# A decoder layer with a mixture of experts: the last three scatters patched by marking matrices counted per token tile, and a fourth tile read before the last scatter

## The chip, the cores and the metric

The kernel runs on one core of a Trainium2 chip. The metric is the device time of one execution in microseconds (us), as the median of three runs.

## The reference

One layer on x of shape (1, 1024, 1024), all float32: attention, then a hierarchical mixture of experts, then a final norm. What matters here is its end:

```python
gates = jnp.sum(jax.nn.one_hot(eid, N_EXPERTS) * top_w[..., None], axis=1)   # two experts of 32 per token
y = jnp.zeros_like(h)
for e in range(N_EXPERTS):
    hid = jax.nn.silu(jnp.dot(h, w_gate[e])) * jnp.dot(h, w_up[e])
    y = y + gates[:, e:e + 1] * jnp.dot(hid, w_down[e])
x = x + gate_m[:, None] * y
...
return rms_norm(x, g_final)
```

Each token's row of 1024 values goes to two experts, and the final norm needs both results of a token.

## The kernel before

The 1024 tokens are 8 token tiles of 128 rows (tile 0 to tile 7). After attention and routing, the work on the experts goes in `NSTEP` = 20 steps, called lists here. A list holds up to 128 rows, in four groups of 32, for one to four experts. For list n, GpSimd (POOL) gathers the rows of the tokens from memory (`gather`, line 760), TensorE (PE) turns them and multiplies them with the weights (`turn_rows`, `gate_up`, `turn_hidden`, `down_proj`), ScalarE (ACT) and VectorE (DVE) evacuate, `ev_y` on DVE (lines 1603 and 1606) weighs the result and adds the token's x where this is its first expert, and POOL scatters the rows into the table `expert_rows` in memory (`scatter`, line 767). The table (`y_dram`) has 2048 rows: one for each token's first expert, and one for its second.

At the end, the two rows of each token are read back, added, normed and written to the output. Most tiles do this by DMA: two reads of 512 KB by `expert_rows` (line 617), an addition on DVE (`combine`, line 1691), the sum of squares on ACT (line 1080), a small addition and a power of -0.5 on POOL (lines 826 and 827), the scaling on DVE (`finish`, line 1700), and a write of 512 KB from SyncE (SP, line 664). These reads wait for `rows_out`, which POOL raises once every scatter has landed.

Tiles 0, 1 and 2 (`AHEAD` = 3) don't wait for the last three lists, 17, 18 and 19 (`NLATE` = 3, `LATE` = 17). Their rows are read once the scatters up to list 16 have landed (line 630), while lists 18 and 19 are still being computed. Their rows in lists 17 to 19 aren't scattered (the index is set out of bounds). Instead, PE adds them: for each such tile and late list, DVE makes a 128x128 matrix of zeros and ones (a mark, line 1664), and a product of the mark with the list's rows, which are still in SBUF, puts each row at its token (`add_into`, line 2222). A product with the identity adds the rows that were read, once DVE has added their two halves (line 1685). Sum of squares and scaling of these tiles read PSUM. They are the tiles in `mixed`.

The order of the end is written out by hand: `read` is the order of the reads behind `rows_out`, `last` the order in which ACT, POOL and the writes of SP take the tiles, and a list of calls at line 1703 the order of `combine` and `finish` on DVE. Each engine runs its instructions in the order of the program, and SP's queue holds both the reads and the writes of the output.

Of the kernel before, what the change touches and what calls it, by code (L numbers as in the profile page):

```python
# [11 lines left out]
ALU = mybir.AluOpType  # L12
# [53 lines left out]
def hybrid_layer(nc, x, c, w_ada, b_ada, g_attn, w_in, g_kv, w_uk, w_uv, lam_q1, lam_k1, lam_q2, lam_k2,  # L66
# [88 lines left out]
    with ctx:  # L155
# [153 lines left out]
        def dist(t):  # L309
# [83 lines left out]
        marks = [mark_room[NLATE * i:NLATE * (i + 1)] for i in range(AHEAD)]  # L393
        zero_rows = W7[:, D:2 * D]
        iota_tok = BIAS[:, 2, 0:P]
        late_tok = logits[:, :, :].rearrange("p t n -> p (t n)")[:, 2 * NT + 5 * T + NLATE:2 * NT + 5 * T + NLATE * (1 + AHEAD)].rearrange(
            "p (i j) -> p i j", j=NLATE)
# [63 lines left out]
        def scattered(b):  # L461

            return len(range(b, LATE, 2))
# [14 lines left out]
        def _(sp):  # L478
# [140 lines left out]
            for n in range(NSTEP + 1):  # L619
# [4 lines left out]
                if n >= 1:  # L624
# [16 lines left out]
            with sp.If(n_ov > 0):  # L641
# [12 lines left out]
                sp.wait_ge(yg_ahead, 64 * AHEAD)  # L654
# [14 lines left out]
        def _(pool):  # L669
# [94 lines left out]
            def scatter(n):  # L764

                pool.wait_ge(y_sb, 2 * n + 2)
                pool.indirect_dma_start(out=y_dram, out_offset=bass.IndirectOffsetOnAxis(
                                            ap=dst_rows[:, n:n + 1].bitcast(U32), axis=0), in_=held[n % HELD], in_offset=None,
                                        bounds_check=2 * S - 1, oob_is_err=False
                                        ).then_inc(y_out[n % 2] if n < LATE else y_last, 16)  # L770
# [31 lines left out]
            pool.wait_ge(yg_ahead, 32 * AHEAD)  # L802
# [5 lines left out]
            with pool.If(n_ov > 0):  # L808
# [3 lines left out]
                pool.wait_ge(y_last, 16 * NLATE)  # L812
# [8 lines left out]
            pool.wait_ge(y_last, 16 * NLATE)  # L821
# [9 lines left out]
        def _(act):  # L831
# [238 lines left out]
            for n, t in enumerate(last):  # L1070
                if t in mixed:
                    i = mixed.index(t)
                    act.wait_ge(mix_ps, i + 1)
                    whole = PS[:, 2 * i:2 * i + 2, :].rearrange("p a n -> p (a n)")
# [10 lines left out]
        def _(dve):  # L1085
# [566 lines left out]
            for n in range(NSTEP):  # L1652
# [9 lines left out]
                if 3 <= n < 3 + NLATE * AHEAD:  # L1662
# [593 lines left out]
```

## Time and profile before

| | |
|---|---|
| time, median of 3 runs | 997.08 us (996.19 to 998.70) |
| the profiled execution's own time | 995.87 us |
| its span in the trace | 994.1 us |
| granted TensorE clock, mean | 0.992 of full speed |
| busy: PE, DVE, ACT, POOL | 947.6, 630.1, 398.3, 120.3 us |

The span runs from the first instruction to the last. The profiled execution took 1.8 us more than its span, and it was 1.2 us under the median. Busy shares are of the whole span, while all that the change moves at the end lies in the last 50 us.

### The profile page before, as it was taken

Reading aid. Unit: us, or ns where it says so; the run is one execution under the profiler, and the core shown is the slowest. Engines: PE = TensorE matmul, PEld = TensorE weight load, DVE = VectorE, ACT = ScalarE, POOL = GpSimd, SP = SyncE. Lnnn points to the kernel's source line nnn. Section 1 sums busy time; section 2 is a strip of 40 time slices with the busy share of each in tenths; the row PEclk is TensorE's granted clock in tenths of the full one; section 3 lists DMA queues with packets and bytes.
Section 4 is the critical chain, followed back from the end, with each engine's and each line's share of the span. In section 5 each row is a group of like instructions: output and inputs, shape, how many; then the busy total and the mean of one; then the engine's idle time right before and its main releaser. Section 6 shows DMA issues by size and latency. Waiting matters only on the chain.

```text
span 994.1 us, 15197 instructions
## 1 busy us (share of the span) xinstructions
PE 947.6 (95%) x5400; PEld 520.1 (52%) x5400; DVE 630.1 (63%) x1670; ACT 398.3 (40%) x901; POOL 120.3 (12%) x221
## 2 busy tenths in 40 slices
PE   3899999999999999999999999999899999999895
PEld 2455476444446856667776555555634433344342
DVE  3378646999999799887777423345724444444356
ACT  6131134676671188877668412121211221111103
POOL 2101000000005711110000000000111111111114
PEclk9899999999999999999999999999999999999998
DMA  9998100101103100040000410059899999999979
GB/s 324 328 358 298 43 22 22 44 21 43 43 22 107 69 1 1 2 171 23 2 2 1 156 57 37 27 212 404 312 411 421 393 423 420 420 420 421 420 307 372
DMA packets 70093, 188.37 MB, mean 189 GB/s; under 512 B 10280, under 2 KB 37216, under 8 KB 57728
## 3 DMA queue, kind: packets, MB, share of 16 engines
q1 hardware_dynamic: 61888, 169.48, 44.6%
q0 software_dynamic: 5760, 16.33, 4.2%
q10 hardware_dynamic: 2368, 1.57, 0.5%
q8 instruction: 44, 0.72, 0.3%
q14 instruction: 33, 0.27, 0.1%
HBM read 169.98 MB, written 22.04 MB: 193 GB/s over the span
## 4 chain that ended last, share of the span: by engine, by line
PE 53%; DVE 20%; DMA 16%; issue 6%; POOL 3%; ACT 1%; SPq 0%; DVEq 0%; POOLq 0%; ACTq 0%
DMA expert_rows<-HT,SC 12%; PE PS L2018 11%; DVE BIAS L1222 8%; PE PS L1911 6%; PE PS L2148 5%; PE PS L1954 5%; PE PS L1976 4%; PE PS L1872 3%; PE PS L2171 3%; PE PS L1824 3%; PE PS L1971 2%; DVE X L1286 2%; PE PS L1849 2%; PE PS L1789 2%; DMA HT<-h_rows,SC 2%
## 5 line engine op out<-in xcount | busy, mean ns | idle before, releaser
L1824 PE MATMUL PS<-HT,X 128*128 128x512 f32 x384 | 168.8, 593 | 0.0
L1824 PEld LDWEIGHTS PS<-HT,X 128*128 128x128 f32 x384 | 72.5, 190 | 92.4 <-issue 92.2
L936 ACT ACTIVATE X<-X,nmx 128x128 f32<-128x128 f32 (+7 forms) x128 | 98.4, 770 | 51.7 <-DVE nmx L1286 51.4
L2018 PE MATMUL PS<-QKV,HT 128*128 128x512 f32 x256 | 113.7, 597 | 0.0
L1222 DVE TENSOR_SCALAR_CACHE_REDUCE BIAS<-SC,W 128x384 f32<-128x384 f32 (+3 forms) x128 | 96.4, 810 | 1.1
L2148 PE MATMUL PS<-QKV,HT 128*32 128x512 f32 (+1 forms) x528 | 91.9, 594 | 2.8 <-ACT HT L1034 1.2
L919 ACT ACTIVATE X<-SC,W 128x896 f32<-128x896 f32 x64 | 69.6, 1088 | 43.1 <-DVE W L1210 43.1
L1594 DVE TENSOR_TENSOR HT<-PS,HT 128x256 f32<-128x256 f32 x20 | 8.5, 425 | 123.3 <-ACT HT L1042 123.3
L1911 PE MATMUL PS<-QKV 64*128 64x512 f32 (+3 forms) x384 | 79.0, 517 | 1.6 <-DVE nmx L1286 1.1
L2018 PEld LDWEIGHTS PS<-QKV,HT 128*128 128x128 f32 x256 | 47.4, 190 | 53.7 <-issue 53.6
L1954 PE MATMUL PS<-ident,X 128*128 128x128 f32 x432 | 63.2, 279 | 2.2 <-DVE X L1304 2.1
L1042 ACT ACTIVATE HT<-PS 128x256 f32<-128x256 f32 x20 | 7.7, 383 | 132.2 <-PE PS L2148 125.5
L1286 DVE CUSTOM_DVE_ANT_0 X<-PS,R 128x128 f32<-128x128 f32 (+7 forms) x80 | 50.8, 674 | 14.6 <-PE PS L1911 8.6
L2148 PE MATMUL PS<-SC,HT 128*32 128x512 f32 (+1 forms) x160 | 56.4, 593 | 0.0
L1286 DVE CUSTOM_DVE_ANT_0 X<-PS,SC 128x1024 f32<-128x1024 f32 (+5 forms) x48 | 42.0, 887 | 17.9 <-PE PS L1911 17.8
L1954 PEld LDWEIGHTS PS<-ident,X 128*128 128x128 f32 x432 | 47.3, 141 | 11.4 <-issue 8.6
L1911 PEld LDWEIGHTS PS<-QKV 64*128 64x128 f32 x384 | 31.6, 185 | 27.8 <-issue 20.6
L2148 PEld LDWEIGHTS PS<-QKV,HT 128*32 128x32 f32 (+1 forms) x528 | 24.6, 111 | 36.9 <-issue 34.0
L760 POOL DMA_INDIRECT HT<-h_rows,SC x20 | 20.6, 1029 | 188.9 <-DMA expert_rows<-HT,SC 132.2
L1114 DVE SCALAR_TENSOR_TENSOR QKV<-QKV,cact 128x512 f32<-128x512 f32 x56 | 42.1, 752 | 2.0
L1971 PEld LDWEIGHTS PS<-QKV,HT 128*128 128x128 f32 x288 | 34.5, 191 | 16.6 <-issue 9.2
L2148 PE MATMUL PS<-X,HT 128*32 128x512 f32 (+1 forms) x112 | 42.3, 593 | 0.0
(335 smaller groups left out, 1590.4 us busy)
## 6 DMA issues: line engine op xcount, KB each, us to landing
QKV<-in_w_down_dram SPq DMA_DIRECT2D x20, 1024.0 KB, 26.4
QKV<-in_w_gate_dram SPq DMA_DIRECT2D x19, 1024.0 KB
QKV<-in_w_up_dram SPq DMA_DIRECT2D x19, 1024.0 KB
QKV<-in_w_ada_dram SPq DMA_DIRECT2D x8, 2048.0 KB, 12.7
QKV<-in_w_ada_dram SPq DMA_DIRECT2D x8, 1024.0 KB, 12.5
X<-in_w_in_dram SPq DMA_DIRECT2D x16, 512.0 KB, 3.8
X<-in_w_down_dram SPq DMA_DIRECT2D x8, 1024.0 KB
W<-in_w_gate_dram SPq DMA_DIRECT2D x5, 1024.0 KB
```

Source lines behind the costliest of these rows:

```text
L919: act.activation(RL[:, n % 2, 0:w], SC[:, sc_off[t]:sc_off[t] + w], ACT.Sign, bias=tk[:, 4, i:i + 1].bitcast(F32), scale=-1.0, accum_out=c ...
L936: act.activation(sc, sc, ACT.Exp, bias=nmx[:, i % 4, m:m + 1], scale=-1.0, accum_out=rs[:, i, m:m + 1]).then_inc(exp_done, 1)
L1114: link(dve.scalar_tensor_tensor(out=w[:, 0, :], in0=w[:, j, :], scalar=cact[:, j:j + 1], in1=w[:, 0, :], op0=ALU.mult, op1=ALU.add))
L1222: dve.tensor_scalar(BIAS[:, i % 3, 0:w], SC[:, sc_off[t]:sc_off[t] + w], thr.bitcast(F32)[:, i:i + 1], 0.0, ALU.is_lt, ALU.add, accum_out= ...
L1286: dve.tensor_tensor_reduce(sc_buf[i % 4][:, m, 0:w], PS[:, 2 * m:2 * m + 2, :].rearrange("p a n -> p (a n)")[:, BANK * n:BANK * n + w], aw ...
L1824: end = pe.matmul(PS[:, 2 * b + half, :], WS[:, b, j, :], HT[:, j, BANK * half:BANK * (half + 1)], start=(j == 0), stop=(j == KC - 1))
L1911: end = pe.matmul(PS[:, 2 * m + n + c0 // BANK, 0:c1 - c0], QKV[rows_m, q0:q0 + P], QKV[rows_m, k0 + c0:k0 + c1], start=True, stop=True)
L1954: end = pe.transpose(PS[:, 4 + g % 2, c0:c0 + P], sc_buf[i % 4][:, m, P * b:P * (b + 1)], ident[:, :])
L1971: end = pe.matmul(PS[:, 6 + h % 2, slot], turned_at(i)[:, g % 4, P * (b - b0):P * (b - b0 + 1)], vf[:, u * S + P * b:u * S + P * (b + 1)], ...
L1976: end = pe.matmul(PS[DH * m:DH * (m + 1), 6 + h % 2, slot], vd[:, b, v0:v0 + DH], turned_at(i)[:, g % 4, c0:c0 + P], start=(b == 0), stop= ...
L2018: end = pe.matmul(PS[:, n % 4, :], HT[:, k, P * (n // 2):P * (n // 2 + 1)], wo[:, k, BANK * (n % 2):BANK * (n % 2 + 1)], start=(k == 0), s ...
L2148: end = pe.matmul(PS[at, 2 + b, :], hgT[b][:, P * c_ + at.start:P * c_ + at.stop], WGU[w][:, c_, :, :], start=(c_ == 0), stop=(c_ == KC - 1))
```

## The change

Marks are now counted per tile. `first_late` = (0, 1, 1, 2) gives for tiles 0 to 3 the first late list that is patched by a mark: tile 0 has marks for lists 17, 18 and 19, tiles 1 and 2 for lists 18 and 19, tile 3 for list 19 alone. These are 8 marks instead of 9. Tiles 1 and 2 are read after scatter 17 has landed, tile 3 after scatter 18, and tile 3 is then combined on DVE as before, and only then completed in PSUM by PE. The scatters of lists 17 and 18 count on the alternating semaphores, and each waits for the scatter two before it. `last`, `mixed` and the order of calls on DVE are new.

```diff
-        AHEAD, NLATE = 3, 3
+        AHEAD, NLATE, PATCHED = 3, 3, 4
+        first_late = (0, 1, 1, 2)
-        last = (0, 3, 4, 1, 5, 6, 2, 7)
-        mixed = (0, 1, 2)
+        last = (0, 4, 1, 5, 3, 6, 2, 7)
+        mixed = (0, 1, 3, 2)
...
         def scattered(b):
-            return len(range(b, LATE, 2))
+            return len(range(b, NSTEP - 1, 2))
...
-            for t in range(AHEAD):
+            for t in range(PATCHED):
                 for k in range(2):
                     row = S * k + P * t
                     sp.dma_start(y_dram[row:row + P, :], zero_rows).then_inc(yg_ahead, 16)
...
                     if n == LATE:
                         for b in range(2):
-                            sp.wait_ge(y_out[b], 16 * scattered(b))
+                            sp.wait_ge(y_out[b], 16 * len(range(b, LATE, 2)))
                         for t in range(AHEAD):
-                            expert_rows(t, yg_ahead)
+                            if first_late[t] == 0:
+                                expert_rows(t, yg_ahead)
+                    if n == LATE + 1:
+                        sp.wait_ge(y_out[1], 16 * scattered(1))
+                        for t in range(AHEAD):
+                            if first_late[t] == 1:
+                                expert_rows(t, yg_ahead)
...
             sp.sem_inc(tables_set, 1)
+            sp.wait_ge(y_out[0], 16 * scattered(0))
+            for t in range(AHEAD, PATCHED):
+                expert_rows(t, yg_in[read.index(t)])
             sp.wait_ge(rows_out, 1)
-            for i, t in enumerate(read):
-                expert_rows(t, yg_in[i])
+            for t in range(PATCHED, T):
+                expert_rows(t, yg_in[read.index(t)])
...
                 pool.wait_ge(y_sb, 2 * n + 2)
+                if LATE <= n < NSTEP - 1:
+                    pool.wait_ge(y_out[n % 2], 16 * (n // 2))
...
-            link(dve.tensor_scalar(late_dst, PS[:, 2, LATE:NSTEP], P * AHEAD + 0.5, None, ALU.is_ge))
+            for j in range(NLATE):
+                link(dve.tensor_scalar(late_dst[:, j:j + 1], PS[:, 2, LATE + j:LATE + j + 1], P * tiles_of[j] + 0.5, None,
+                                       ALU.is_ge))
...
-            link(dve.tensor_copy(late_tok[:, 0, :], PS[:, 2, LATE:NSTEP]))
-            for i in range(1, AHEAD):
-                link(dve.tensor_scalar(late_tok[:, i, :], PS[:, 2, LATE:NSTEP], float(-P * i), None, ALU.add))
+            for i, f in enumerate(first_late):
+                link(dve.tensor_scalar(late_tok[:, tok_col[i]:tok_col[i] + NLATE - f], PS[:, 2, LATE + f:NSTEP], float(-P * i),
+                                       None, ALU.add))
...
             finish(0)
             combine(3)
             combine(4)
+            finish(4)
+            combine(5)
+            finish(1)
+            finish(5)
+            combine(6)
             finish(3)
-            combine(5)
-            finish(4)
-            finish(1)
-            combine(6)
-            finish(5)
+            finish(6)
             combine(7)
-            finish(6)
             finish(2)
             finish(7)
...
-            for i in range(AHEAD):
-                for j in range(NLATE):
-                    pe.wait_ge(marked, NLATE * i + j + 1)
+            pe.wait_ge(marked, len(mark_of))
+            for t in mixed:
+                for j in range(first_late[t], NLATE):
                     pe.wait_ge(y_sb, 2 * (LATE + j + 1))
-                    add_into(i, marks[i][j], held[(LATE + j) % HELD], j == 0, False)
-                pe.wait_ge(marked, NLATE * AHEAD + i + 1)
-                add_into(i, ident[:, :], yg[i][0], False, True).then_inc(mix_ps, 1)
+                    add_into(mix_banks[t], marks[(t, j)], held[(LATE + j) % HELD], j == first_late[t], False)
+                if t < AHEAD:
+                    pe.wait_ge(marked, len(mark_of) + t + 1)
+                else:
+                    pe.wait_ge(cb_done, read.index(t) + 1)
+                add_into(mix_banks[t], ident[:, :], yg[t][0], False, True).then_inc(mix_ps, 1)
```

SP's queue, from the last weight load to the first write of the output, the part for more than the planned rows left out. `X<-expert_rows` are reads of tiles 0 to 2, `QKV<-expert_rows` those of tiles 3 to 7, `y_out0` and `y_out1` count the landed scatters of even and odd lists. Before:

```order
L450 DMA QKV<-in_w_down_dram 128x2048
L617 DMA X<-expert_rows 128x1024 [waits dn_ps,y_out0,gu_ps,y_out1]
L617 DMA X<-expert_rows 128x1024 x5
L634 TENSOR_LOAD ovi [waits dn_ps,gu_ps,route_done]
...
L617 DMA QKV<-expert_rows 128x1024 [waits rows_out]
L617 DMA QKV<-expert_rows 128x1024 x9
L664 DMA out_dram<-X 128x1024 [waits fin_done]
```

And now:

```order
L455 DMA QKV<-in_w_down_dram 128x2048
L622 DMA X<-expert_rows 128x1024 [waits dn_ps,y_out0,gu_ps,y_out1]
L622 DMA X<-expert_rows 128x1024
L622 DMA X<-expert_rows 128x1024 [waits y_out1,dn_ps,gu_ps]
L622 DMA X<-expert_rows 128x1024 x3
L645 TENSOR_LOAD ovi [waits dn_ps,route_done,gu_ps]
...
L622 DMA QKV<-expert_rows 128x1024 [waits y_out0]
L622 DMA QKV<-expert_rows 128x1024
L622 DMA QKV<-expert_rows 128x1024 [waits rows_out]
L622 DMA QKV<-expert_rows 128x1024 x7
L678 DMA out_dram<-X 128x1024 [waits fin_done]
```

Four of the six early reads moved behind a wait for scatter 17, and two of the ten late reads moved ahead of `rows_out`, behind a wait for scatter 18.

DVE's queue at the end, from `finish(0)` on. `TENSOR_TENSOR QKV<-QKV` is a `combine` (yg_in0 to yg_in4 are tiles 3 to 7), `SCALAR_TENSOR_TENSOR` a `finish`, from PSUM where PS stands as its input. Before:

```order
L1700 SCALAR_TENSOR_TENSOR X<-PS,ss,HT 128x1024 [waits rstd_done,act_in]
L1691 TENSOR_TENSOR QKV<-QKV 128x1024 [waits yg_in0]
L1691 TENSOR_TENSOR QKV<-QKV 128x1024 [waits yg_in1]
L1700 SCALAR_TENSOR_TENSOR QKV<-QKV,ss,HT 128x1024 [waits rstd_done]
L1691 TENSOR_TENSOR QKV<-QKV 128x1024 [waits yg_in2]
L1700 SCALAR_TENSOR_TENSOR QKV<-QKV,ss,HT 128x1024 [waits rstd_done]
L1700 SCALAR_TENSOR_TENSOR X<-PS,ss,HT 128x1024 [waits rstd_done]
L1691 TENSOR_TENSOR QKV<-QKV 128x1024 [waits yg_in3]
L1700 SCALAR_TENSOR_TENSOR QKV<-QKV,ss,HT 128x1024 [waits rstd_done]
L1691 TENSOR_TENSOR QKV<-QKV 128x1024 [waits yg_in4]
L1700 SCALAR_TENSOR_TENSOR QKV<-QKV,ss,HT 128x1024 [waits rstd_done]
L1700 SCALAR_TENSOR_TENSOR X<-PS,ss,HT 128x1024 [waits rstd_done]
```

And now:

```order
L1717 SCALAR_TENSOR_TENSOR X<-PS,ss,HT 128x1024 [waits rstd_done,act_in]
L1709 TENSOR_TENSOR QKV<-QKV 128x1024 [waits yg_in0]
L1709 TENSOR_TENSOR QKV<-QKV 128x1024 [waits yg_in1]
L1717 SCALAR_TENSOR_TENSOR QKV<-QKV,ss,HT 128x1024 [waits rstd_done]
L1709 TENSOR_TENSOR QKV<-QKV 128x1024 [waits yg_in2]
L1717 SCALAR_TENSOR_TENSOR X<-PS,ss,HT 128x1024 [waits rstd_done]
L1717 SCALAR_TENSOR_TENSOR QKV<-QKV,ss,HT 128x1024 [waits rstd_done]
L1709 TENSOR_TENSOR QKV<-QKV 128x1024 [waits yg_in3]
L1717 SCALAR_TENSOR_TENSOR QKV<-PS,ss,HT 128x1024 [waits rstd_done]
L1717 SCALAR_TENSOR_TENSOR QKV<-QKV,ss,HT 128x1024 [waits rstd_done]
L1709 TENSOR_TENSOR QKV<-QKV 128x1024 [waits yg_in4]
L1717 SCALAR_TENSOR_TENSOR X<-PS,ss,HT 128x1024 [waits rstd_done]
```

In both, one more row follows, `finish(7)`. Before, the `finish` behind the first two combines was that of tile 3, and `finish(6)` and `finish(2)` stood between `combine(7)` and `finish(7)`. Now the first is that of tile 4, and only `finish(2)` stands between `combine(7)` and `finish(7)`.

## Rows read from the trace of the kernel before

**Rows 1.** The page's first line:

```profile
span 994.1 us, 15197 instructions
```

**Rows 2.** The chain that ended last, in order of time: start us, us, what:

```profile
963.82 3.35 DMA expert_rows<-HT,SC
...
976.12 1.16 ACT HT L1080 x2
```

**Rows 3.** Timeline of DVE at the end: start us, us, engine line op, idle before:

```profile
963.89 3.50 DVE L1685 TENSOR_TENSOR X<-X 128x1024 f32<-128x1024 f32 x3 [0.85 <-issue]
970.50 1.28 DVE L1700 SCALAR_TENSOR_TENSOR X<-PS,ss,HT 128x1024 f32<-128x1024 f32 x1 [3.11 <-POOL ss L827]
972.30 1.23 DVE L1691 TENSOR_TENSOR QKV<-QKV 128x1024 f32<-128x1024 f32 x1 [0.52 <-DMA QKV<-expert_rows]
974.87 1.23 DVE L1691 TENSOR_TENSOR QKV<-QKV 128x1024 f32<-128x1024 f32 x1 [1.33 <-DMA QKV<-expert_rows]
976.54 1.28 DVE L1700 SCALAR_TENSOR_TENSOR QKV<-QKV,ss,HT 128x1024 f32<-128x1024 f32 x1 [0.45 <-POOL ss L827]
977.74 1.22 DVE L1691 TENSOR_TENSOR QKV<-QKV 128x1024 f32<-128x1024 f32 x1
...
981.12 1.28 DVE L1700 SCALAR_TENSOR_TENSOR X<-PS,ss,HT 128x1024 f32<-128x1024 f32 x1 [0.44 <-POOL ss L827]
...
989.49 1.27 DVE L1700 SCALAR_TENSOR_TENSOR QKV<-QKV,ss,HT 128x1024 f32<-128x1024 f32 x1
```

**Rows 4.** Timeline of POOL at the end:

```profile
977.35 0.52 POOL L826 TENSOR_TENSOR ss<-ss,eps_row 128x1 f32<-128x1 f32 x1 [0.85 <-ACT HT L1080]
977.95 1.41 POOL L827 TENSOR_TENSOR ss<-ss,neghalf 128x1 f32<-128x1 f32 x1
...
981.32 0.54 POOL L827 TENSOR_TENSOR ss<-ss,neghalf 128x1 f32<-128x1 f32 x1
```

**Rows 5.** Stretches of the end: busy us by engine, PEclk, DMA share, GB/s:

```profile
963.50:967.30 3.80, 3.80 (x10) 1.66 (x9) 3.41 (x3) 0.00 (x0) 0.97 (x1) 1.00 0.15 54
...
972.30:980.00 7.70, 7.70 (x19) 3.42 (x18) 5.48 (x5) 4.42 (x8) 4.13 (x6) 1.00 1.02 408
```

**Rows 6.** DMA issues of 990.5 to 991, KB each, us to landing:

```profile
out_dram<-QKV SPq DMA_DIRECT2D x1, 512.0 KB, 2.9
```

**Rows 7.** Timeline of SP's queue:

```profile
948.46 3.11 SPq L617 DMA_DIRECT2D X<-expert_rows  x6
967.32 4.97 SPq L617 DMA_DIRECT2D QKV<-expert_rows  x10
...
990.80 0.33 SPq L664 DMA_DIRECT2D out_dram<-QKV  x1
```

**Rows 8.** Timeline, scatters of lists 17 and 18:

```profile
948.38 0.97 POOL L767 DMA_INDIRECT expert_rows<-HT,SC  x1 [13.06 <-DVE HT L1606]
...
959.24 0.97 POOL L767 DMA_INDIRECT expert_rows<-HT,SC  x1 [9.89 <-DVE HT L1606]
```

**Rows 9.** DMA issues of 946 to 957, us to landing:

```profile
expert_rows<-HT,SC POOLq DMA_INDIRECT x1, 7.7
```

**Rows 10.** DMA issues of 957 to 961, us to landing:

```profile
expert_rows<-HT,SC POOLq DMA_INDIRECT x1, 5.0
```

**Rows 11.** DMA issues of 951 to 952, us to landing:

```profile
X<-expert_rows SPq DMA_DIRECT2D x2, 512.0 KB, 10.1
```

**Rows 12.** Timeline of PE behind the last list:

```profile
961.30 5.31 PE L2222 MATMUL PS<-HT,BIAS 128*128 128x512 f32 x12
966.45 1.88 PE L2222 MATMUL PS<-X,ident 128*128 128x512 f32 x4
...
980.18 1.88 PE L2222 MATMUL PS<-X,ident 128*128 128x512 f32 x4
```

**Rows 13.** What SP's queue waited for, 310 to 700: us, times, longest:

```profile
SPq L552 <- PE PS L1911: 108.7, 1, 108.7
```

**Rows 14.** Timeline of DVE where the lists are set up:

```profile
713.47 0.35 DVE L1631 TENSOR_SCALAR logits<-PS 128x3 f32<-128x3 f32 x2
715.74 0.41 DVE L1616 TENSOR_SCALAR HT<-PS,gm,modc 128x128 f32<-128x128 f32 x1 [1.91 <-PE PS L2135]
```

**Rows 15.** Waits of 957 to 994.1, us in total, times, longest:

```profile
DVE QKV L1691 <- DMA QKV<-expert_rows: 1.9, 2, 1.3
```

More of the change, by code:

```diff
@@ L392, in hybrid_layer @@
         mark_room = [BIAS[:, 2, P * i:P * (i + 1)] for i in range(1, 8)] + [wgr_room[:, P * i:P * (i + 1)] for i in range(2)]
-        marks = [mark_room[NLATE * i:NLATE * (i + 1)] for i in range(AHEAD)]
+        mark_of = [(i, j) for i in range(PATCHED) for j in range(first_late[i], NLATE)]
+        marks = {at: room for at, room in zip(mark_of, mark_room)}
+        tok_col = [mark_of.index((i, first_late[i])) for i in range(PATCHED)]
+        tiles_of = [sum(1 for f in first_late if f <= j) for j in range(NLATE)]
+        assert len(mark_of) <= len(mark_room)
+        mix_banks = [2 * (i % 4) for i in range(PATCHED)]
         zero_rows = W7[:, D:2 * D]
         iota_tok = BIAS[:, 2, 0:P]
-        late_tok = logits[:, :, :].rearrange("p t n -> p (t n)")[:, 2 * NT + 5 * T + NLATE:2 * NT + 5 * T + NLATE * (1 + AHEAD)].rearrange(
-            "p (i j) -> p i j", j=NLATE)
+        late_tok = logits[:, :, :].rearrange("p t n -> p (t n)")[:, 2 * NT + 5 * T + NLATE:2 * NT + 5 * T + NLATE + len(mark_of)]
         late_dst = logits[:, :, :].rearrange("p t n -> p (t n)")[:, 2 * NT + 5 * T:2 * NT + 5 * T + NLATE]
@@ L653, in _ @@
                 sp.wait_ge(rows_out, 1)
-                sp.wait_ge(yg_ahead, 64 * AHEAD)
+                sp.wait_ge(yg_ahead, 32 * PATCHED + 32 * AHEAD)
                 for t in range(AHEAD):
@@ L801, in _ @@
             pool.wait_ge(route_done, 2)
-            pool.wait_ge(yg_ahead, 32 * AHEAD)
+            pool.wait_ge(yg_ahead, 32 * PATCHED)
             for n in range(NSTEP):
@@ L820, in _ @@
                 pool.wait_ge(y_out[b], 16 * scattered(b))
-            pool.wait_ge(y_last, 16 * NLATE)
+            pool.wait_ge(y_last, 16)
             pool.sem_inc(rows_out, 1)
@@ L1073, in _ @@
                     act.wait_ge(mix_ps, i + 1)
-                    whole = PS[:, 2 * i:2 * i + 2, :].rearrange("p a n -> p (a n)")
+                    whole = PS[:, mix_banks[t]:mix_banks[t] + 2, :].rearrange("p a n -> p (a n)")
                 else:
@@ L1661, in _ @@
                     dve.wait_ge(tables_set, 2 * NE + 2)
-                if 3 <= n < 3 + NLATE * AHEAD:
-                    i, j = divmod(n - 3, NLATE)
-                    dve.tensor_scalar(marks[i][j], iota_tok, late_tok[:, i, j:j + 1], None, ALU.is_equal).then_inc(marked, 1)
+                if 3 <= n < 3 + len(mark_of):
+                    dve.tensor_scalar(marks[mark_of[n - 3]], iota_tok, late_tok[:, n - 3:n - 2], None,
+                                      ALU.is_equal).then_inc(marked, 1)
             dve.wait_ge(route_done, 2)
@@ L1669, in _ @@
                     dve.wait_ge(y_out[b], 16 * scattered(b))
-                dve.wait_ge(y_last, 16 * NLATE)
+                dve.wait_ge(y_last, 16)
                 place_overflow()
@@ L1682, in _ @@
             dve.wait_ge(tables_set, 2 * NE + 3)
-            dve.wait_ge(yg_ahead, 64 * AHEAD)
+            dve.wait_ge(yg_ahead, 32 * PATCHED + 32 * AHEAD)
             for t in range(AHEAD):
@@ L1696, in finish @@
                 if t in mixed:
-                    i = mixed.index(t)
-                    whole = PS[:, 2 * i:2 * i + 2, :].rearrange("p a n -> p (a n)")
+                    whole = PS[:, mix_banks[t]:mix_banks[t] + 2, :].rearrange("p a n -> p (a n)")
                 dve.wait_ge(rstd_done, rstd_out + last.index(t) + 1)
@@ L2217, in _, with add_into @@
                             down_proj(n, over(b), [(b, 0, 4)], [(b, came(DNS))])
-            def add_into(i, stationary, rows, start, stop):
+            def add_into(bank, stationary, rows, start, stop):
                 for h in range(2):
-                    end = pe.matmul(PS[:, 2 * i + h, :], stationary, rows[:, BANK * h:BANK * (h + 1)], start=start,
+                    end = pe.matmul(PS[:, bank + h, :], stationary, rows[:, BANK * h:BANK * (h + 1)], start=start,
                                      stop=stop)
                 return end
-            for i in range(AHEAD):
-                for j in range(NLATE):
-                    pe.wait_ge(marked, NLATE * i + j + 1)
+            pe.wait_ge(marked, len(mark_of))
+            for t in mixed:
+                for j in range(first_late[t], NLATE):
                     pe.wait_ge(y_sb, 2 * (LATE + j + 1))
-                    add_into(i, marks[i][j], held[(LATE + j) % HELD], j == 0, False)
-                pe.wait_ge(marked, NLATE * AHEAD + i + 1)
-                add_into(i, ident[:, :], yg[i][0], False, True).then_inc(mix_ps, 1)
+                    add_into(mix_banks[t], marks[(t, j)], held[(LATE + j) % HELD], j == first_late[t], False)
[4 more added lines that the diff above has]
+                add_into(mix_banks[t], ident[:, :], yg[t][0], False, True).then_inc(mix_ps, 1)
 _INS = ["x", "c", "w_ada", "b_ada", "g_attn", "w_in", "g_kv", "w_uk", "w_uv", "lam_q1", "lam_k1", "lam_q2", "lam_k2",
```

4 lines of the change are left out of this document (2 added, 2 removed).

## The prediction

> **What bounds the kernel now.** I read the page first. PE is busy for 95% of a span of 994.1 us [rows 1], but that average says nothing here: the change touches a few small instructions at 317 and 713 us, and the last 50 us. So I followed the chain of work that ended last through those. Up to 963.8 us it runs through the lists on PE, which keep their order, and then comes what can move. Scatter 19 starts at 963.82 and has landed 3.35 us later [rows 2]. SP starts ten reads at 967.32 [rows 7]. The first pair has landed when DVE starts `combine(3)` at 972.30, and the second at 974.87; only these two combines wait for a DMA, 1.9 us in all [rows 3, 15]. From 974.87 on, DVE goes back and forth with ACT and POOL, until `finish(7)` ends at 989.49 + 1.27 = 990.76 [rows 3]. SP writes that tile at 990.80, and the write lands 2.9 us later [rows 6, 7]. So the reader should see two things. The tail starts bound by reads, for 1.9 us, and ends bound by an order of short dependent steps. DMA is almost idle while scatter 19 is under way (share 0.15) and full afterwards (1.02 at 408 GB/s) [rows 5].
>
> **The steps of the tail.** What one tile costs in dependent steps I take from its rows. Combine(4) starts at 974.87; its square starts at 976.12, 1.25 later; POOL's addition starts at 977.35, 1.23 later [rows 2 to 4]. The power starts some 0.26 after an addition that isn't held, and takes 0.54 where it isn't held [rows 4]; the next finish follows some 0.04 later. Sum from a combine's start to its own finish's start: 1.25 + 1.23 + 0.26 + 0.54 + 0.04 = 3.32 us. It is longer where DVE works from SBUF meanwhile: the power from 977.95 took 1.41 and ended 0.40 after combine(5) did (977.74 + 1.22), whereas that from 981.32, beside a finish that reads PSUM, took 0.54 [rows 3, 4]. On DVE, what follows a finish starts 1.20 after it (976.54 to 977.74), and what follows a combine 1.13 after it (three such additions take 3.50) [rows 3].
>
> **The change, part by part.**
>
> *Set-up.* Two more writes of zeros on SP: the queue then waits 108.7 us for attention [rows 13], which hides them; uncovered they would cost some 2 us. On DVE, three more tiny operations at 713 us, at 0.35 for two about 0.5 us, before a wait of 1.91 for PE [rows 14]. One mark fewer. All this at nothing.
>
> *Scatters 17 and 18 wait for scatters 15 and 16.* SP started its early reads at 948.46, once scatters up to 16 had landed, and scatter 17 started at 948.38 [rows 7, 8]. So both waits are over by then, give or take 0.1 us. The next scatter, 18, has 9.89 us of idle time ahead of it [rows 8]. Nothing.
>
> *Reads of tiles 1 and 2 behind scatter 17.* It landed at 948.38 + 7.7 = 956.1 [rows 8, 9], beside six reads. It now also moves the rows of tiles 1 and 2 (two eighths of at most 128 rows of 4 KB, some 0.1 MB), but has only two reads beside it, so I take 956 again. The four reads carry 2.1 MB, at 408 GB/s 5.1 us. A pair at the end took 5.0 us from issue to landing (967.32 to 972.3) for 1.05 MB, or 2.6 us of data [rows 3, 5, 7], so 2.4 us are start and landing. So they land at 956.1 + 5.1 + 2.4 = 963.6, and with the gain of the final norm (512 KB, 1.3 us), which is loaded at the same time, at 964.9. The old ones were there at about 951.1 + 10.1 = 961.2 [rows 7, 11]. Late next is the addition of the halves at 963.89 (it waits for all three tiles). Behind it PE waits: tile 0's identity product, first matmul at 966.45, needs the first sum, done at about 965.1 [rows 3, 12]. Leave 0.4 for its weight load, and there is about 1.0 us of slack: the loss is between 0 and 0.2, and I take 0.
>
> A rule of the Trainium skill, "DMA: Bandwidth & Descriptors" (Anatomy of one DMA), gives a transfer about 2.0 us plus its bytes over 436 GB/s, mostly for the receipt of its write. By it alone an estimate for the four reads would be 6.8 us, and they would be there at 962.9, without any loss; the sum would be the same, and only the slack differ. The rows' 2.4 us are used.
>
> *PE.* Before, 3 tiles of 3 marks and an identity, 24 matmul instructions; now 3 + 2 + 1 + 2 marks and four identities, again 24. The rows show each as two records, six instructions from start to start in some 5.15 us, so 0.86 each [rows 12]. Tile 0 is ready at 968.3 as before, tile 1 six instructions later (973.5), tile 3 four later (976.9), tile 2 six later (982.1), each before ACT takes it in the order below.
>
> *Tile 3 read ahead.* Scatter 18 lands at 959.24 + 5.0 = 964.2 [rows 8, 10], or up to 1 us later behind the moved reads. SP then reads tile 3 in a stretch where DMA is idle [rows 5]. It lands by 970.3 (5.0 after 965.3), and `combine(3)` no longer waits: it starts behind `finish(0)`, 970.50 + 1.20 = 971.70. Scatter 19 (about 0.2 MB) shares the engines with it for a while and lands 0 to 0.9 us later. So `rows_out` comes at 967.2 to 968.1, and tile 4, now first in line, lands 5.0 later: 972.3 to 973.2 instead of 974.87. I take 973.0. The bound from the other side, where all 1.05 MB go ahead of scatter 19, is 2.6 later, 974.8. From below, combine(4) can't start before 971.70 + 1.13 = 972.83.
>
> *The new order.* This is where I expect the 1.9 us to go. From combine(4) at 973.0: nothing stands on DVE between it and its own finish, so `finish(4)` at 976.3 (3.32 later). Before, `finish(3)` came 1.67 us behind combine(4). `combine(5)` 977.5. Power 1 is held by it: 977.5 + 1.23 + 0.41 + 0.04, `finish(1)` 979.2 (from PSUM, holds nobody). `finish(5)` is 3.32 behind its combine: 980.8. `combine(6)` 982.0. Power 3 is held: `finish(3)` 983.7. `finish(6)` 3.32 behind its combine: 985.4. `combine(7)` 986.6. Power 2 is held: `finish(2)` 988.2. `finish(7)` 3.32 behind its combine: 989.9, ends at 991.15. Before, combine(7) had `finish(6)` and `finish(2)` to cover its steps; now it has one.
>
> So from combine(4)'s start to finish(7)'s start are 16.9 us, all dependent. Finish(7) ends at 991.15 instead of 990.76: +0.4 us. Every us that tile 4 lands later than 972.8 counts in full, every us earlier nothing. The reads of tiles 5 to 7 (975.6, 978.2, 981 with the writes) are all there before their combines. The last write takes 2.9 us again.
>
> **The sum.** Span 994.1 + 0.4 = 994.5; the execution's own time 995.87 + 0.4 = 996.3. The median of the runs shown is 997.08, so I forecast 997.5 us.
>
> **The rivals.**
>
> *The order is harmless and the reads' gain stays (faster).* For it: 1.9 us of waits for reads [rows 15], and DMA at 1.02 of its capacity from 972.3 to 980 [rows 5], of which 1.05 MB now go earlier, worth 2.6 us. If the tail is bound by transfers rather than steps, it gets between 1.9 and 2.6 us: 995.2 to 994.5. Against it: the last write landed 2.9 after its issue, which leaves no queue to relieve, and after 974.87 no DVE wait was for a read [rows 3, 6]. It needs ACT and POOL steps shorter than the rows have them. Chance 0.17.
>
> *Scatter 19 is held by tile 3's reads (slower).* They are issued about when the scatter is, on the same DMA engines. With the whole 2.6 us ahead of it, `rows_out` comes at 969.8, tile 4 at 974.8, and finish(7) 2.0 later than at 972.8: with the order's price +2.2, 999.3 us. It decides from tile 4 landing later than 973; it passes 0.3% if that is later than 975.6. For it: scatters among reads took 7.7 and 5.0 us instead of 3.35 [rows 2, 9, 10]. Against it: it has little to move, and both flow at once. Chance 0.20.
>
> *My own case,* tile 4 at 972.3 to 974, 997.2 to 998.5: chance 0.60. The remaining 0.03 are for something elsewhere.
>
> **How the numbers follow.** The three runs of before spread over 2.5 us, so 0.3% (3 us, 994.1 to 1000.1) is about what can be told from no change. The faster rival's far bound, 994.5, doesn't pass it; with the spread of a median it may: 0.05. The slower rival passes it in about a third of its cases (with late sums of tiles 1 and 2 on top): 0.08. Within 0.3%: 0.87. The range takes in most of both rivals: 994.9 to 999.6. My own case by itself has 996.9 to 998.7.
>
> **What would show it.** Right: combine(3) behind finish(0) without a DMA wait; combine(4) at about 973; an idle DVE of some 2 us ahead of finish(4), and 0.4 to 1.0 us ahead of nearly every later finish; finish(7) ending at 991 with only finish(2) between it and combine(7). Scatter 19 to landing 3.4 to 4.3 us. The additions of the halves start at 964 to 965. Wrong: combine(4) still at 974.9 or later, with `rows_out` late (slower rival), or finish(7) ending before 990 (faster rival). The forecast as a whole would be wrong if the lists themselves took another time, which nothing here moves.

## The result, and the profile after

The changed kernel takes 997.65 us (median of 20 runs, 993.82 to 999.70), the kernel before 995.16 us in the 20 runs beside it (990.93 to 998.70). The ratio is 1.0026, with a 95% interval from 1.0015 to 1.0037: a loss of 2.6 us, clear of zero and, by its middle, just inside the 0.3% of the prediction's "within". The profiled execution took 995.41 us of its own, with a span of 993.6 us.

A single execution of either kernel lies within some 4 us of its median. So spans of two executions can't be compared to one us, and the readings below compare the same stretch in each: the **tail**, from the end of the last evacuation of list 19 on DVE (before: line 1606, at 963.05 us) to the end of the last finish. In the kernel before it is 990.76 - 963.05 = 27.7 us [rows 3].

The timeline of DVE in the changed kernel, over its tail. Line 1622 is the last evacuation, 1703 the additions of halves, 1709 `combine`, 1717 `finish`:

```profile
957.97 0.75 DVE L1622 SCALAR_TENSOR_TENSOR HT<-HT,logits,PS 128x512 f32<-128x512 f32 x1
...
963.12 3.50 DVE L1703 TENSOR_TENSOR X<-X 128x1024 f32<-128x1024 f32 x3 [4.40 <-DMA X<-expert_rows]
970.02 1.28 DVE L1717 SCALAR_TENSOR_TENSOR X<-PS,ss,HT 128x1024 f32<-128x1024 f32 x1 [3.41 <-POOL ss L843]
971.22 2.35 DVE L1709 TENSOR_TENSOR QKV<-QKV 128x1024 f32<-128x1024 f32 x2
975.68 1.28 DVE L1717 SCALAR_TENSOR_TENSOR QKV<-QKV,ss,HT 128x1024 f32<-128x1024 f32 x1 [2.11 <-POOL ss L843]
976.88 1.22 DVE L1709 TENSOR_TENSOR QKV<-QKV 128x1024 f32<-128x1024 f32 x1
978.53 1.28 DVE L1717 SCALAR_TENSOR_TENSOR X<-PS,ss,HT 128x1024 f32<-128x1024 f32 x1 [0.43 <-POOL ss L843]
...
989.26 1.28 DVE L1717 SCALAR_TENSOR_TENSOR QKV<-QKV,ss,HT 128x1024 f32<-128x1024 f32 x1 [0.39 <-POOL ss L843]
```

The tail is now 990.54 - 958.72 = 31.8 us, 4.1 longer. It splits at the start of combine(4) (the second of the two at 971.22, 1.13 later, so 972.35). Up to there it was 974.87 - 963.05 = 11.8 us and is 13.6; from there to the start of finish(7) it was 14.6 and is 16.9. Finish(7), without idle time ahead of it in the last of [rows 3], now has 0.39 of it like nearly every finish.

Up to combine(4), the additions, which started 0.84 us after the last evacuation [rows 3], start 4.40 after it, and what ended that wait was a read of tiles 1 and 2. SP's queue in the changed kernel:

```profile
944.41 9.51 SPq L622 DMA_DIRECT2D X<-expert_rows  x6
963.53 5.01 SPq L622 DMA_DIRECT2D QKV<-expert_rows  x10
```

Against [rows 7], the six early reads are drawn out over 9.5 us, and the ten late ones still leave in one go: the two of tile 3 start at 963.53, and `rows_out` comes before they have been issued. The DMA issues of 952 to 957 (scatter 18) and of 957 to 961 (scatter 19), us to landing:

```profile
expert_rows<-HT,SC POOLq DMA_INDIRECT x1, 8.6
...
expert_rows<-HT,SC POOLq DMA_INDIRECT x1, 4.5
```

Scatter 18, issued at 954.91, landed 8.6 us later, at 963.5, against 5.0 in the kernel before [rows 10]. Scatter 19, issued at 959.49, landed at 964.0.

TensorE, over the same time:

```profile
956.97 5.31 PE L2239 MATMUL PS<-HT,BIAS 128*128 128x512 f32 x12
964.39 3.45 PE L2239 MATMUL PS<-X,ident 128*128 128x512 f32 x4 [2.11 <-DVE X L1703]
967.63 3.88 PE L2239 MATMUL PS<-HT,BIAS 128*128 128x512 f32 x8
```

The identity product of tile 0, without a pause before and 1.88 us long [rows 12], waits 2.11 us for the additions and then takes 3.45. The stretches show why (the third number from the right is the granted clock):

```profile
963.00:965.00 2.00, 0.61 (x1) 0.30 (x2) 1.89 (x2) 0.00 (x0) 0.00 (x0) 0.94 0.27 64
965.00:967.00 2.00, 2.00 (x4) 0.89 (x3) 1.61 (x2) 0.00 (x0) 0.00 (x0) 0.50 0.96 340
967.00:969.00 2.00, 2.00 (x4) 0.84 (x4) 0.00 (x0) 1.11 (x2) 0.00 (x0) 0.71 1.02 393
```

Behind the idle time, TensorE ran at 0.50 of full speed (1.2 GHz) and got back to 2.4 GHz some 3 us later. The share of 0.71 is a mean of both levels. That puts finish(0) 6.9 us behind the start of the additions, where it was 6.6 with no wait [rows 3] and 5.4 in three traces below (x1_split, x2_cover, x9_gain_again) that had a wait of over 3 us and kept the clock. So finish(0) came 1.5 us late by it.

Not all of that reaches combine(4), which needs its own read too. The DMA issue of 964.88 to 965.23, the second read of tile 4, us to landing:

```profile
QKV<-expert_rows SPq DMA_DIRECT2D x1, 512.0 KB, 6.3
```

It landed at about 971.2. Without the slow clock combine(4) could have started then instead of at 972.35, so the clock took about 1.2 us of this execution (an estimate), and the stretch up to combine(4) would have been 12.5 us, still 0.7 longer than before.

### The profile page after: what moved, and what is told of

Its sections match the earlier page's. It is cut to its first block, busy times and chain, and to the rows that moved or that the text cites. A ratio compares the mean times of both kernels' runs of the same rounds, so it can differ in the third digit from the quotient of the medians.

```text
span 993.6 us, 15195 instructions
## 1 busy us (share of the span) xinstructions
PE 946.7 (95%) x5400; PEld 517.7 (52%) x5400; DVE 630.4 (63%) x1672; ACT 398.1 (40%) x901; POOL 120.2 (12%) x221
## 4 chain that ended last, share of the span: by engine, by line
PE 63%; DVE 21%; DMA 7%; issue 5%; ACT 2%; POOL 1%; SPq 1%; POOLq 0%; DVEq 0%; ACTq 0%
PE PS L2035 11%; PE PS L2165 11%; DVE BIAS L1238 8%; PE PS L1928 6%; PE PS L2188 5%; PE PS L1971 5%; PE PS L1993 4%; DMA X<-in_w_down_dram 3%; PE PS L1889 3%; PE PS L1841 3%; DMA expert_rows<-HT,SC 2%; PE PS L1988 2%; DVE X L1302 2%; PE PS L1866 2%; PE PS L1806 2%
## 5 line engine op out<-in xcount | busy, mean ns | idle before, releaser
L1302 DVE CUSTOM_DVE_ANT_0 X<-PS,R 128x128 f32<-128x128 f32 (+7 forms) x80 | 50.8, 674 | 14.6 <-PE PS L1928 8.6
## 6 DMA issues: line engine op xcount, KB each, us to landing
QKV<-in_w_down_dram SPq DMA_DIRECT2D x20, 1024.0 KB, 26.5
QKV<-in_w_ada_dram SPq DMA_DIRECT2D x8, 2048.0 KB, 14.6
QKV<-in_w_ada_dram SPq DMA_DIRECT2D x8, 1024.0 KB, 12.7
X<-in_w_down_dram SPq DMA_DIRECT2D x8, 1024.0 KB, 28.1
```

What stands on the lines that cost most here:

```text
L1302: dve.tensor_tensor_reduce(sc_buf[i % 4][:, m, 0:w], PS[:, 2 * m:2 * m + 2, :].rearrange("p a n -> p (a n)")[:, BANK * n:BANK * n + w], aw ...
```

## The experiments

Each was timed in turn with the kernel before, 6 to 12 runs each. The other columns are from one profiled execution each: the tail by the definition above, the time from the last evacuation to the end of the span (which takes in the last write), and DVE's idle time ahead of the additions.

| run | what it is | ratio to the kernel before (95%) | tail us | to the span's end us | wait ahead of the additions us |
|---|---|---|---|---|---|
| (before) | | 1 | 27.7 | 31.0 | 0.85 |
| (changed) | | 1.0026 (1.0015 to 1.0037) | 31.8 | 34.9 | 4.40 |
| x1_split | before, tiles 1 and 2 read behind scatter 17 | 1.0022 (1.0009 to 1.0035) | 28.8 | 32.0 | 3.64 |
| x7_order | before, with the new order | 1.0021 (1.0007 to 1.0034) | 30.4 | 33.4 | 0.85 |
| x2_cover | changed, combines earlier | 1.0011 (0.9999 to 1.0024) | 28.1 | 32.4 | 4.00 |
| x3_early | changed, tiles 0 to 2 read at the old place | 1.0013 (1.0002 to 1.0024) | 28.6 | 31.7 | 0.84 |
| x4_gain, x9_gain_again | changed, gain loaded later | 1.0039 (1.0024 to 1.0055), 1.0024 (1.0009 to 1.0038) | 29.4, 31.7 | 32.4, 34.7 | 1.06, 3.21 |
| x8_warm | changed, extra work on TensorE | 1.0051 (1.0031 to 1.0070) | 33.2 | 36.2 | 3.56 |
| x5_before_order | before, another order | 0.9998 (0.9985 to 1.0011) | 26.4 | 30.8 | 0.84 |
| x6_both, x10_both_again | early reads, tile 3 ahead, order with cover | 0.9989 (0.9973 to 1.0004), 0.9997 (0.9982 to 1.0013) | 26.4, 26.5 | 29.5, 29.6 | 0.84, 0.85 |

A ratio is good to some 1.1 to 2 us, so the difference of two ratios only to some 1.6 us or more. What lies under that is read from the traces. The time to the span's end moves with the ratio, within 1.3 us in every kernel but x4_gain.

**x1_split: the late reads alone.**

```diff
 (the kernel before)
+        first_late = (0, 1, 1)
...
-                        for t in range(AHEAD):
-                            expert_rows(t, yg_ahead)
+                        expert_rows(0, yg_ahead)
+                    if n == LATE + 1:
+                        sp.wait_ge(y_out[1], 16 * scattered(1))
+                        for t in range(1, AHEAD):
+                            expert_rows(t, yg_ahead)
...
 (and the marks and semaphore counts that follow from it)
```

> The kernel before with one part of the change alone: tile 0 is still read once the scatters up to 16 have landed, tiles 1 and 2 only behind scatter 17; three patched tiles, the old order of the end, all ten late reads behind rows_out. My theory (the early reads of tiles 1 and 2 come too late): VectorE waits 3 to 4 us for them ahead of the first addition of halves; the tail, from the end of the last list's evacuation on VectorE to the end of the last finish, grows from 27.7 us to 29.5 to 30 us, of which 1.9 us of the lateness are absorbed by waits for reads that vanish; the time is 1.8 to 2.3 us over that of the kernel before. Rival (the whole loss is the new order of the end): the tail stays at 27.7 and the time within 0.5 us of the kernel before.

Measured: 1.0022, 2.2 us over the kernel before, and a wait of 3.64 us:

```profile
963.56 3.50 DVE L1695 TENSOR_TENSOR X<-X 128x1024 f32<-128x1024 f32 x3 [3.64 <-DMA X<-expert_rows]
```

The time is as expected, but the tail is only 1.1 us longer, at 28.8 us instead of 29.5 to 30. The rival falls by the ratio, whose interval starts at 1.0009: the loss isn't the order's alone.

The trace doesn't bear out the path that I had in mind. Its chain of work that ended last, in order of time:

```profile
960.69 4.06 DMA expert_rows<-HT,SC
...
966.22 6.35 DMA QKV<-expert_rows
...
972.59 1.24 DVE QKV L1701
```

It doesn't go through the late additions. They push finish(0) and combine(3) back, but combine(4), at 972.59, still waits 1.18 us for its read. It stands 12.7 us behind the last evacuation instead of 11.8, and what holds it there is scatter 19, which landed after 4.06 us instead of 3.35 [rows 2], so that the reads behind it started later. The moved reads were in flight beside it until 963.5. So in this trace they cost most of their 1 us through a scatter. Where a second us of the ratio comes from isn't shown; the interval takes in both.

**x7_order: the order alone.**

```diff
 (the kernel before)
-        last = (0, 3, 4, 1, 5, 6, 2, 7)
+        last = (0, 4, 1, 5, 3, 6, 2, 7)
...
 (and the changed kernel's list of combine and finish)
```

> The kernel before with only the changed kernel's order of the end: the order of tiles on ScalarE, GpSimd and SyncE, and the calls of combine and finish on VectorE; three tiles patched, all six early reads at the old place, all ten late reads behind rows_out. My theory (the order alone costs a chain of dependent steps, 16.9 us from combine(4)'s start to finish(7)'s start, and combine(4) can't start earlier here): the tail, from the end of the last list's evacuation to the end of the last finish, is 30.3 us instead of 27.7, and the time 2.3 to 2.6 us over that of the kernel before. Rival (the end is bound by transfers, the order has slack): within 0.7 us of the kernel before.

Measured: 1.0021, 2.1 us over. In the timeline of its DVE:

```profile
974.94 1.22 DVE L1691 TENSOR_TENSOR QKV<-QKV 128x1024 f32<-128x1024 f32 x1 [1.40 <-DMA QKV<-expert_rows]
978.27 1.28 DVE L1700 SCALAR_TENSOR_TENSOR QKV<-QKV,ss,HT 128x1024 f32<-128x1024 f32 x1 [2.11 <-POOL ss L827]
...
992.19 1.29 DVE L1700 SCALAR_TENSOR_TENSOR QKV<-QKV,ss,HT 128x1024 f32<-128x1024 f32 x1 [0.91 <-POOL ss L827]
```

From combine(4) to finish(7) are 17.3 us; the tail is 30.4, expected 30.3. The idle 2.11 us ahead of finish(4) stand in every kernel with this order. So the steps do bound the end. By the ratios either part alone costs nearly what the whole change does, 2.2 and 2.1 us of 2.6, but the intervals are too wide to say whether parts add up. By the tails they are 1.1 and 2.7 us of 4.1, of which about 1.2 are the slow clock, so the order is the larger part.

**x2_cover: the changed kernel with combines one place earlier.**

```diff
             finish(0)
             combine(3)
             combine(4)
+            combine(5)
             finish(4)
-            combine(5)
+            combine(6)
             finish(1)
             finish(5)
-            combine(6)
+            combine(7)
             finish(3)
             finish(6)
-            combine(7)
             finish(2)
             finish(7)
```

> The changed kernel with only the calls on VectorE in another order: finish(0), combine(3), combine(4), combine(5), finish(4), combine(6), finish(1), finish(5), combine(7), finish(3), finish(6), finish(2), finish(7); the order of the tiles on ScalarE, GpSimd and SyncE is unchanged. My theory (from combine(4) on the new order is a chain of dependent steps with nothing to cover them): from combine(4)'s start to finish(7)'s start it takes 13.8 us instead of 16.9, the tail falls from 31.8 to 28.7 us and the time by 2.5 to 3.1 us against the changed kernel, to or just under the kernel before. Rival (transfers bound the end: reads and writes at full rate): the finishes move but the last write lands later after its issue than 2.9 us, and the time falls by under 1 us.

Measured: 1.0011, so 1.5 us under the changed kernel's ratio (not clear of zero), with a tail of 28.1. From combine(4) at 973.13 to finish(7) at 986.96 are 13.8 us, as expected, and DVE goes from finish to finish almost without a pause. But two combines wait for reads (combine(4) 1.14 us), and of the expected 2.5 to 3.1 us about half are seen:

```profile
975.69 1.22 DVE L1709 TENSOR_TENSOR QKV<-QKV 128x1024 f32<-128x1024 f32 x1 [1.34 <-DMA QKV<-expert_rows]
...
983.37 1.28 DVE L1717 SCALAR_TENSOR_TENSOR QKV<-PS,ss,HT 128x1024 f32<-128x1024 f32 x1
984.57 1.27 DVE L1717 SCALAR_TENSOR_TENSOR QKV<-QKV,ss,HT 128x1024 f32<-128x1024 f32 x1
985.76 1.28 DVE L1717 SCALAR_TENSOR_TENSOR X<-PS,ss,HT 128x1024 f32<-128x1024 f32 x1
986.96 1.27 DVE L1717 SCALAR_TENSOR_TENSOR QKV<-QKV,ss,HT 128x1024 f32<-128x1024 f32 x1
```

The rival was right on the rest. The last write, issued in 988.2 to 992, took 3.9 us to land instead of 2.9 [rows 6]:

```profile
out_dram<-QKV SPq DMA_DIRECT2D x1, 512.0 KB, 3.9
```

Under the steps lies a second bound, the transfers: this write ends the span 4.4 us behind the last finish, where it was 3.1 in the changed kernel.

**x3_early: early reads at the old place.**

```diff
-        first_late = (0, 1, 1, 2)
+        first_late = (0, 0, 0, 2)
 (and a tenth mark in a buffer that is free by then, and tile 3's reads wait for scatters 17 and 18)
```

> The changed kernel with tiles 0, 1 and 2 all read at the old place, once the scatters up to 16 have landed (each is patched for lists 17, 18 and 19, so ten marks instead of eight, and four more matmul instructions, 3.4 us, at the end of TensorE), tile 3 still patched for list 19 and read behind scatter 18, the new order of the end. My theory: the additions of halves start 0.85 us after the last evacuation again instead of 4.4, the tail falls from 31.8 to 28.1 to 28.8 us, the time by 3.0 to 3.7 us against the changed kernel, and scatter 18 lands in some 5 us, so that tile 3 is read 3 us before the others. Rival (the new order is all): the sums start early but the tail stays above 31.

Measured: 1.0013, 1.3 us under the changed kernel's ratio (not clear of zero); expected were 3.0 to 3.7. The tail did what was expected, 28.6 us, with the additions on time and scatter 18 landed in 4.9 us. The larger number had been worked out from the changed kernel's profiled execution, whose 31.8 us held about 1.2 us of slow clock. Tile 3's reads started at 966.20, behind scatter 18 alone, and combine(4) 10.4 us after the last evacuation, instead of 11.8 before: the read ahead does gain 1.4 us once nothing stands in its way.

**x4_gain and x9_gain_again: the gain out of the way.**

```diff
+            act.wait_ge(yg_ahead, 32 * PATCHED + 32 * AHEAD)
             act.dma_start(gfin, g_final.partition_broadcast(P)).then_inc(act_in, 16)
```

> The changed kernel, but the load of the final norm's gain (512 KB on ScalarE's queue), which was issued together with the reads of tiles 1 and 2, waits until these have landed. My theory: the reads land about 1.3 us earlier (7 to 8 us instead of 9.5 for the last), scatter 18 too, so that the wait ahead of the additions shrinks from 4.4 to some 3 us and the time falls by 1 to 1.5 us against the changed kernel. Rival (the reads are late only because scatter 17 lands late, and the gain shares nothing with them): no difference, or a loss where the gain itself then comes too late for the first finish.

> The same kernel as x4_gain (the gain's load waits for the reads of tiles 1 and 2), again, since its trace has a tail 2.5 us shorter than that of the changed kernel while its six runs were 0.39% over the kernel before. If the tail in the trace is typical, the ratio to the kernel before is 1.001 to 1.002; if the late gain costs something in most executions, it is again 1.003 or more.

Inconclusive. The wait was 1.06 us in one profiled execution and 3.21 in the other, and the ratios, 1.0039 over six runs and 1.0024 over twelve, are not clearly below the changed kernel's. The four reads did come in sooner without the gain beside them: 8.4 and some 10 us from the first issue to the last landing, against 10.4 to 11.0 in the four traces with it (changed, x1_split, x2_cover, x8_warm). But the gain is now loaded beside the late reads, and there combine(4) waits 1.30 and 1.33 us for its read. So the gain makes up at most a part of the lateness, and moving it moves the wait. With the two traces of this one kernel 2.3 us apart, a single tail is good to about 1 or 2 us.

**x8_warm: TensorE kept at work.**

```diff
+                if t == 0:
+                    for _ in range(12):
+                        pe.matmul(PS[:, 7, 0:2 * P].rearrange("p (a n) -> p a n", a=2), ident[:, :],
+                                  ident[:, :].unsqueeze(1).to_broadcast([P, 2, P]), start=True, stop=True)
```

> The changed kernel with twelve extra matmuls (128x256, into a PSUM bank not yet in use) on TensorE between tile 0's last mark and its identity product, where the trace of the changed kernel has TensorE idle for 2.1 us and then at half clock (four records in 3.45 us instead of 1.88). Theory: the idle wait brings the clock down, and the extra work keeps it up: the identity product takes 1.9 us, finish(0) comes 5.4 us after the start of the additions instead of 6.9, and the time falls by up to 1.5 us in executions like the profiled one, less in the median. Rival (the clock falls whatever TensorE does there, or the wait is mostly too short to matter): no change of the median, or a small loss where the extra work outlasts the wait (it takes some 2.6 us).

Measured: 1.0051, a loss. The extra work took twice what I had reckoned:

```profile
963.56 5.34 PE L2250 MATMUL PS<-ident 128*128 128x256 f32 x24
968.74 1.88 PE L2239 MATMUL PS<-X,ident 128*128 128x512 f32 x4
```

Twelve instructions are 24 records, and they ran 3.8 us beyond the first addition (done at 964.9). The clock stayed at 1.00, but it does so in three other traces that have such a wait and no extra work (x1_split, x2_cover, x9_gain_again), so this says nothing on the clock. It shows the price of a late tile 0: its product 3.7 us later than in x2_cover, by the start of the additions, cost a further 2.5 us over the changed kernel in the ratio, a difference barely clear of zero.

**x5_before_order: a looser order in the kernel before.**

```diff
-        last = (0, 3, 4, 1, 5, 6, 2, 7)
+        last = (0, 3, 1, 4, 5, 2, 6, 7)
...
             combine(5)
-            finish(4)
             finish(1)
+            finish(4)
             combine(6)
-            finish(5)
             combine(7)
-            finish(6)
+            finish(5)
             finish(2)
+            finish(6)
             finish(7)
```

> The kernel before with another order of the end: tiles 0, 3, 1, 4, 5, 2, 6, 7, and on VectorE finish(0), combine(3), combine(4), finish(3), combine(5), finish(1), finish(4), combine(6), combine(7), finish(5), finish(2), finish(6), finish(7). By steps alone the last finish ends 1.9 us earlier (tail 25.9 us instead of 27.7). Theory that steps alone bound the end: the time falls by 1.5 to 1.9 us. Rival (under the steps lie the transfers: 9.4 MB behind rows_out at 0.41 MB per us are over only some 23 us later): the last finish ends earlier, but its write lands 4 to 5 us after its issue instead of 2.9, and the time falls by under 0.8 us. I hold the rival likelier, since the last write took 3.9 us where the order was loosened in the changed kernel.

Measured: 0.9998. The last finish ends 1.3 us earlier in its tail (1.9 by steps alone; combine(7) waits 0.99 us for its read), and the last write, issued at 989.5, lands 4.0 us later instead of 2.9. The rival holds: the transfers take back what the steps give, and from the last evacuation to the span's end are 30.8 us where there were 31.0.

**x6_both and x10_both_again: the parts put together otherwise.** The kernel of x3_early, with `last` = (0, 4, 1, 5, 3, 6, 7, 2) and this order on DVE:

```diff
             combine(4)
+            combine(5)
             finish(4)
-            combine(5)
+            combine(6)
             finish(1)
+            combine(7)
             finish(5)
-            combine(6)
             finish(3)
             finish(6)
-            combine(7)
-            finish(2)
             finish(7)
+            finish(2)
```

> Tiles 0, 1 and 2 read early at the old place and patched for three lists, tile 3 patched for list 19 and read behind scatter 18 (ten marks), and an order with cover: tiles 0, 4, 1, 5, 3, 6, 7, 2, and on VectorE finish(0), combine(3), combine(4), combine(5), finish(4), combine(6), finish(1), combine(7), finish(5), finish(3), finish(6), finish(7), finish(2). By steps alone the tail is 26.3 us against 27.7 before and 28.5 in the same kernel with the changed kernel's order. Here 1 MB of the reads is out of the way before rows_out, so transfers end some 2.6 us earlier than in the kernel before: my theory gives a time 1 to 1.5 us under that of the kernel before. Rival (tile 3's reads only delay scatter 19 and gain nothing, as the changed kernel's trace has it): the same time as the kernel before or above.

> The same kernel as x6_both, again, since it was the only one whose median was below the kernel before (ratio 0.9989 with an interval from 0.9973 to 1.0004). Theory: the ratio is 0.9985 to 0.9990 again, 1 to 1.5 us under the kernel before. Rival: chance, and the ratio comes out at 1.000 or above.

Measured: 0.9989 and 0.9997. Both profiled executions have tails of 26.4 and 26.5 us, and a last write that lands in 2.7 and 2.6 us, so both bounds moved. In x6_both:

```profile
961.57 6.75 SPq L622 DMA_DIRECT2D QKV<-expert_rows  x10
...
986.15 0.33 SPq L679 DMA_DIRECT2D out_dram<-X  x1
```

```profile
out_dram<-X SPq DMA_DIRECT2D x1, 512.0 KB, 2.7
```

Yet neither interval leaves out 1: the ratios put it 1.1 and 0.3 us under the kernel before. It is about 3 us better than the change as made (1.0026 against 0.9997 and 0.9989; the intervals don't overlap). Whether it beats the kernel before stays open.

## Why the prediction was right or wrong

**The forecast of 997.5 us** is next to the measured 997.65, but partly by luck. It was 0.4 us on top of a median of three runs, 997.08, and the 20 runs put the kernel before at 995.16. The change of +0.4 was 2.2 us too small; "within 0.3%" held, though the interval of the ratio goes up to 0.37%. The +0.4 was a difference of two terms: 2.3 us lost by the order, and 1.9 gained because combine(4) would start at 973.0 instead of 974.87. The first held. The second didn't come at all: in place of 9.95 us behind the last evacuation, combine(4) started 13.6 behind it, later than the 11.8 of the kernel before.

**The new order** was sized right. Foretold: combine(4)'s start to finish(7)'s start 16.9 us, about 2 us idle ahead of finish(4), 0.4 to 1.0 ahead of nearly every later finish. Seen: 16.9, 2.11 and 0.39 to 0.44. Alone it costs 2.1 us (x7_order), in keeping with the 2.3 between 16.9 and 14.6.

**"I take 0" for the reads of tiles 1 and 2** is the step that failed first. I had them land 0.3 us before to 1.0 us after the additions would start, and put the loss between 0 and 0.2 us. The additions started 3.2 to 4.4 us after the last evacuation in five of the six traces with these late reads, and alone the late reads cost 2.2 us by the ratio (0.9 to 3.5) and 1.1 by the tail (x1_split). Two things were left out of that term, and one was priced too low. Left out was scatter 18, which moves its rows over the same DMA engines at the same time. Left out was that four reads of one queue don't come in evenly: in the changed kernel they landed 3.7, 4.6, 5.9 and 9.5 us after their issue. And the gain, priced at 1.3 us, took 9.4 us to land instead of 5.0. The last two of the rows:

```profile
X<-expert_rows SPq DMA_DIRECT2D x1, 512.0 KB, 5.9
...
X<-expert_rows SPq DMA_DIRECT2D x1, 512.0 KB, 9.5
```

I had 5.1 + 2.4 from the first issue to the last landing, and 1.3 more with the gain, 8.8 in all; from 952.1 to 963.1 it was 11.0. How much each of the three costs isn't shown: with the gain taken away the reads took some 0.5 to 2.5 us less, and the time nothing clear (x4_gain, x9_gain_again). The prediction's other estimate, 6.8 us by the fit of the Trainium skill, "DMA: Bandwidth & Descriptors" (Anatomy of one DMA), for one transfer on its own, was further off; the measured 11.0 us decides. By the Trainium skill, "DMA: Bandwidth & Descriptors" (Queues, rings and completion order), each DMA engine takes turns, packet by packet, between the queues that have work for it; the trace is in keeping with it, as the last read (963.0), the gain (953.9 + 9.4) and scatter 18 (954.91 + 8.6) all landed within 0.5 us of each other.

**Tile 3 read ahead** didn't happen as foretold. I had scatter 18 landed at the old time or up to 1 us later; it took 8.6 us instead of 5.0, and the reads of tile 3 left together with the others. So tile 4 landed at about 971.2, 12.5 us behind the last evacuation instead of the 9.95 of the sum. The gain of 1.9 us appears only with the early reads at their old place, and then as 1.4 (x3_early).

**The slower rival** came nearest. It decided by tile 4 landing later than 973, which is 9.95 us behind the last evacuation; it landed 12.5 behind it, and the rival's price of +2.2 us is close to the measured 2.6. Its cause was named wrongly: it had scatter 19 held by tile 3's reads, and scatter 19 took 4.5 us, just over the 3.4 to 4.3 of my own case. The delay came one scatter earlier: the moved reads came in late together with scatter 18, which tile 3 waits for. Its clause that late sums of tiles 1 and 2 might come on top came true in the changed kernel's profiled execution, where the chain goes through the late additions and the slow product behind them, by about 1.2 us.

**The faster rival** falls for the new order, but was right about what lies beneath: with a looser order the last write takes 3.9 to 4.0 us (x2_cover, x5_before_order), and only the kernel that takes tile 3's reads out of the way as well gets under it (x6_both, x10_both_again).

**The set-up, the waits between scatters and TensorE's count** cost nothing that shows, as foretold. Scatter 17 was issued 0.78 us after its evacuation ended, as before. What I hadn't foreseen on TensorE is the fall of the clock. In how many executions it falls isn't shown.

## What to carry to other kernels

A read moved behind a wait for a transfer must be priced with everything that is in flight then, on all queues, and by its last landing, not by bytes over bandwidth: here 11 us instead of 7.5 to 8.8. An order of short dependent steps over several engines can be worked out from the rows closely (foretold and seen from combine(4) to finish(7): 16.9 and 16.9, 13.8 and 13.8, 16.9 and 17.3), so it should be worked out before it is changed: each tile's addition needs other work on the same engine between it and its own last step. And a wait that grows isn't yet a loss: the additions here came 3 us late, and in x1_split another chain, scatter to read, still ended later. When two bounds lie 1 us apart, as steps and transfers do here, each can be relieved only together with the other.

## What the runs showed of the hardware

After an idle wait of 2.11 us, TensorE's granted clock was 0.50 in the stretch 965 to 967 and 0.71 in the next two us, and the next group of matmuls followed the first four 3.24 us after their start (964.39 to 967.63) instead of 1.72 (966.45 to 968.17 in the kernel before). After waits of 1.35 (x1_split), 1.71 (x2_cover) and 0.92 us (x9_gain_again), it stayed at 1.00. In the tail it was seen in one execution only.

A power of GpSimd on one column takes 0.54 us where it isn't held. Beside a VectorE instruction that reads both inputs from SBUF it takes 1.41 and ends 0.40 us after it (changed kernel: from 977.09 to 978.50, combine(5) to 978.10); beside one that reads PSUM it isn't held (0.54 from 984.16, during finish(3)). The order of the new tail could be worked out from this and the steps' lengths.

Four reads of 512 KB from one queue, beside a 512 KB load of another queue and a scatter, took 11.0 us from the first issue to the last landing (changed kernel), and the scatter 8.6 us instead of 5.0.
